# Quarter-wise loading and a shared k loop for the first two units of a hybrid decoder's input projection

## What is computed

```python
def rmsnorm(x, g):
    return x * lax.rsqrt(jnp.mean(x * x, axis=-1, keepdims=True) + EPS) * g

z = rmsnorm(x, norm_g) @ w_in               # (256 x 1024) @ (1024 x 3080)
q, k, v, o, gi, gf = jnp.split(z, [nq, 2 * nq, 2 * nq + nv, 2 * nq + 2 * nv,
                                   2 * nq + 2 * nv + A_HEADS], axis=-1)
li = softcap(gi + bf[:A_HEADS])                      # input gate, log
lf = jax.nn.log_sigmoid(softcap(gf + bf[A_HEADS:]))  # forget gate, log
# then, per head: cumulative sums of lf, running maxima, exp, and the chunked mixer
```

## Time and profile before

| | |
|---|---|
| median of 3 runs | 766.49 us (765.99 to 766.7) |
| the profiled execution's own time | 766.79 us |
| its span, first to last instruction | 765.1 us |
| PE busy | 752.0 us, 98% of the span |
| PE weight loads busy | 739.6 us, 97% |
| DVE, ACT, POOL busy | 537.5, 457.3, 228.7 us |
| mean granted TensorE clock | 0.994 |
| HBM traffic | 134.54 MB read, 177 GB/s over the span |

### The profile page before, as it was taken

How to read it: one execution, slowest core, us unless ns; L and a number is a source line. 1 busy time by engine, 2 the same in 40 slices (tenths; PEclk the granted TensorE clock), 3 DMA queues, 4 the chain that set the end, 5 groups by cost and what they waited for, 6 DMA issues and landing times.

```text
span 765.1 us, 16972 instructions
## 1 busy us (share of the span) xinstructions
PE 752.0 (98%) x6454; PEld 739.6 (97%) x6454; DVE 537.5 (70%) x993; ACT 457.3 (60%) x605; POOL 228.7 (30%) x186
## 2 busy tenths in 40 slices
PE   8999999999999999999999999999999999999995
PEld 7999999999999999999999999999999999999994
DVE  5784788888888546547746855766788888887452
ACT  6644557665666456448648637746867666665451
POOL 2350235432222522222322321320214222233321
PEclk9999999999999999999999999999999999999998
DMA  9754264756564565854584285384545656554731
GB/s 288 224 170 131 90 201 157 247 167 207 178 218 153 192 197 174 258 164 145 167 252 127 90 278 153 114 253 132 181 140 190 195 193 208 176 179 143 238 100 55
DMA packets 139805, 136.24 MB, mean 178 GB/s; under 512 B 3585, under 2 KB 139089, under 8 KB 139764
## 3 DMA queue, kind: packets, MB, share of 16 engines
q1 hardware_dynamic: 129016, 130.15, 52.7%
q10 hardware_dynamic: 10748, 5.53, 2.8%
HBM read 134.54 MB, written 1.13 MB: 177 GB/s over the span
## 4 chain that ended last, share of the span: by engine, by line
PE 92%; DVE 3%; issue 1%; ACT 1%; DMA 1%; ACTq 0%; POOL 0%; POOLq 0%; DVEq 0%
PE bank L1367 16%; PE bank L1369 15%; PE bank L1368 15%; PE banks L1368 9%; PE banks L1369 9%; PE banks L1367 9%; PE bank L1594 3%; PE bank L1596 3%; PE bank L1595 3%; PE banks L1628 2%; PE banks L1639 2%; PE bank L1399 1%; PE bank L1401 1%; PE bank L1400 1%; DVE wlo L875 1%
## 5 line engine op out<-in xcount | busy, mean ns | idle before, releaser
L472 POOL TENSOR_TENSOR wlo<-raw,whi 128x512 fp32r<-128x512 f32 (+1 forms) x165 | 218.5, 1357 | 501.7 <-ACT whi L515 501.7
L515 ACT ACTIVATE whi<-raw 128x2048 fp32r<-128x2048 f32 (+1 forms) x135 | 238.1, 1764 | 180.1 <-PE bank L1369 92.9
L875 DVE TENSOR_TENSOR wlo<-raw,whi 128x1024 fp32r<-128x1024 f32 x163 | 198.1, 1253 | 7.6 <-ACT whi L515 6.7
L1367 PE MATMUL bank<-xsA,whi 128*128 128x256 f32 x568 | 159.2, 280 | 0.0
L1368 PE MATMUL bank<-xsA,whi 128*128 128x256 f32 x568 | 157.7, 278 | 0.0
L1369 PE MATMUL bank<-xsA,wlo 128*128 128x256 f32 x568 | 157.6, 277 | 0.0
L1367 PE MATMUL bank<-xsB,whi 128*128 128x256 f32 x480 | 134.2, 280 | 0.3 <-DVE wlo L875 0.2
L1369 PE MATMUL bank<-xsB,wlo 128*128 128x256 f32 x480 | 132.6, 276 | 0.0
L1368 PE MATMUL bank<-xsB,whi 128*128 128x256 f32 x480 | 132.6, 276 | 0.0
L1367 PEld LDWEIGHTS bank<-xsA,whi 128*128 128x128 f32 x568 | 107.4, 189 | 1.4 <-DVE xsA L895 0.8
L1368 PEld LDWEIGHTS bank<-xsA,whi 128*128 128x128 f32 x568 | 107.5, 189 | 0.1
(11 more groups left out here) (202 smaller groups left out, 1521.8 us busy)
## 6 DMA issues: line engine op xcount, KB each, us to landing
raw<-in_f_w_up SPq DMA_DIRECT2D x44, 1024.0 KB, 5.1
raw<-in_w_kv SPq DMA_DIRECT2D x24, 1024.0 KB, 5.8
raw<-in_f_w_down SPq DMA_DIRECT2D x16, 1024.0 KB, 5.2
raw<-in_b_w_q SPq DMA_DIRECT2D x12, 1024.0 KB, 5.3
raw<-in_a_w_in SPq DMA_DIRECT2D x10, 1024.0 KB, 5.9
raw<-in_f_w_down SPq DMA_DIRECT2D x8, 768.0 KB, 4.8
Bi<-bias_by_distance ACTq DMA_DIRECT2D x16, 320.0 KB, 4.7
raw<-in_a_w_out SPq DMA_DIRECT2D x4, 1024.0 KB, 5.4
```

The source lines that it names most:

```text
L472: o = g.tensor_tensor(wlo[s][:, ka:kb, :], raw[s][:, ka * CW:kb * CW] .rearrange("p (k c) -> p k c", c=CW), whi[s][:, ka:kb, :].bitcast(F3 ...
L515: o = a.activation(whi[s][:, k0:k1, :], raw[s][:, k0 * CW:k1 * CW] .rearrange("p (k c) -> p k c", c=CW), ACT.Copy)
L875: v.tensor_tensor(wlo[s][:, ka:kb, :], raw[s][:, ka * CW:kb * CW].rearrange("p (k c) -> p k c", c=CW), whi[s][:, ka:kb, :].bitcast(F32), A ...
L1367: t_.matmul(ps, hi_w, hi_x, start=first, stop=False)
```

## The change

- X, unit 0 and unit 1 arrive in quarters of two blocks, in turn (12 loads of 256 KB). ACT and DVE split each quarter when it is there, of both units.
- PE does both units for each block k: 12 matmuls per k, tiles 0 to 3 in banks 0, 1, 2 and 5. Behind them come the sums, then the gate projection, then the bias table.
- The bias table is one matmul, its two left operands and its two right operands being stacked (`om`, `rg`). Their loads, that of `bif` and that of most of `vcols` go on SP behind unit 2's; ACT loads only the eight gain columns of layer 0.
- Unit 2 goes to banks 6 and 7. The first half of its wlo is made by DVE, the second by POOL; all of unit 1's is DVE's.
- WARM is 10. DVE's gate inputs go from unit 2 to unit 1, ahead of unit 3's wlo; the gate scans go ahead of the emptying of both of unit 3's tiles.

```diff
-WARM = 18
+WARM = 10
 PIECE = 2
-SHARE = 7
...
         def in_bank(t):
-            return 5 if t == 3 else t % 3
+            return {3: 5, 4: 6, 5: 7}.get(t, t % 3)
...
+            for j in range(4):
+                sp.dma_start(X[:, 2 * j:2 * j + 2, :], xT[:, 2 * j:2 * j + 2, :])\
+                    .then_inc(x_in[j], 16)
+                sp.dma_start(*cols_k(0, 2 * j, 2 * j + 2))\
+                    .then_inc(first_in[j] if j < 3 else raw_in[0], 16)
+                sp.dma_start(*cols_k(1, 2 * j, 2 * j + 2))\
+                    .then_inc(second_in[j] if j < 3 else raw_in[1], 16)
...
             for u in range(2, 12):
-                if u == 4:
+                if u == 5:
                     sp.wait_ge(share_lo, 1)
                 load(U_IN + u, 0, 0, cols(w_in, u * CW), KD)
+                if u == 2:
+                    sp.dma_start(om[0:BUCKETS, :], onehot).then_inc(c_in, 16)
...
+                    sp.dma_start(bif[:, :], b_if).then_inc(bif_in, 16)
+                    sp.dma_start(vcols[:, V_KV:], vectors[:, V_KV:]).then_inc(v_in, 16)
...
-            lo(1, k0=SHARE)
-            lo(2)
+            lo(2, k0=KD // 2)
...
+            act.wait_ge(va_in, 16)
+            for j in range(4):
+                act.wait_ge(x_in[j], 16)
+                for k in (2 * j, 2 * j + 1):
                     gained(k, ((xsA, V_A),))
+                if j < 3:
+                    first_part(0, j, first_in[j], first_hi)
+                    first_part(1, j, second_in[j], second_hi)
+                else:
+                    hi(0, k0=6)
+                    hi(1, k0=6)
+                if j == 1:
+                    square_in_turn(0)
+                    square_in_turn(1)
+            for k in range(2, KD):
+                square_in_turn(k)
...
+            dve.wait_ge(va_in, 16)
+            for j in range(4):
+                dve.wait_ge(x_in[j], 16)
+                for k in (2 * j, 2 * j + 1):
                     gained(k, k, ((xsA, V_A),))
...
+                first_part(0, j, first_hi, first_lo)
+                first_part(1, j, second_hi, second_lo)
+                if j == 2:
+                    added(0)
+                    added(1)
+            for k in range(2, KD):
                 added(k)
...
             for u in range(12):
-                if u == 2:
+                if u == 1:
                     gate_inputs()
...
-                    if (u, c) == (3, 1):
+                    if (u, c) == (3, 0):
                         gate_scans()
...
+            for k in range(KD):
+                pe.wait_ge(xlo_done, k + 1)
+                for n, lo_part in ((0, first_lo), (1, second_lo)):
+                    if k == 6:
+                        pe.wait_ge(lo_done[n], 2)
+                    elif k % 2 == 0:
+                        pe.wait_ge(lo_part, k // 2 + 1)
+                    for c in range(2):
+                        cs = slice(c * P, (c + 1) * P)
+                        mm = three(bank[in_bank(2 * n + c)][:, 0:S], whi[n][:, k, cs],
+                                   wlo[n][:, k, cs], xsA[:, k, 0, :], xsA[:, k, 1, :], k == 0,
+                                   k == KD - 1)
...
+            sums(0, 7, True)
...
-            for u in range(12):
+            for u in range(2, 12):
                 t = 2 * u
...
+                waits = {2: [(acc_done, 8), (root_done, 1)], 3: [(ev_done, 1), (ev_done, 2)]}\
+                    .get(u, [(ev_done, t + c - 2) for c in range(2)])
```

More of the change, by code:

```diff
@@ L586, in _, with first_part @@
[L586 to L596, removed]
+            def first_part(n, j, landed, done):
+                act.wait_ge(landed, 16)
+                a.activation(whi[n][:, 2 * j:2 * j + 2, :], raw[n][:, 2 * j * CW:(2 * j + 2) * CW]
+                             .rearrange("p (k c) -> p k c", c=CW), ACT.Copy).then_inc(done, 1)
@@ L1386, in unit @@
                 for k, c in order:
[L1387 removed]
+                    if not begun and k - k0 >= KD // 2:
                         pe.wait_ge(lo_done[s], 2 * rnd(n, i, step) + 2)
@@ L1446, in _ @@
+            sums(0, 7, True)
+            pe.wait_ge(wgl_done, 1)
+            for k in range(KD):
+                for part in range(2):
+                    mm = t_.matmul(bank[3][:, 0:S], wg4[:, k, :, :].rearrange("p j c -> p (j c)"),
+                                   xsA[:, k, part, :], start=k == part == 0,
+                                   stop=k == KD - 1 and part == 1)
+            mm.then_inc(gates_ps, 1)
             pe.wait_ge(c_in, 64)
-            t_.matmul(bank[4][0:NG * BH, 0:DIST], rb[:, :], oh[:, :], start=True, stop=False)
@@ L1448, in _ @@
-            t_.matmul(bank[4][0:NG * BH, 0:DIST], gs[:, :], mk[:, :], start=False, stop=True)\
+            t_.matmul(bank[4][0:NG * BH, 0:DIST], rg[:, :], om[:, :], start=True, stop=True)\
                 .then_inc(bt_done, 1)
-            for u in range(12):
+            for u in range(2, 12):
                 t = 2 * u
-                if u == 1:
-                    pe.wait_ge(share_lo, 1)
-                waits = [(ev_done, t + c - 2) for c in range(2)]
-                if u == 1:
-                    unit(U_IN + 1, xsA, [in_bank(2), in_bank(3)], part=(0, 2))
-                    pe.wait_ge(wgl_done, 1)
-                    for k in range(KD):
-                        for part in range(2):
-                            mm = t_.matmul(bank[3][:, 0:S],
-                                           wg4[:, k, :, :].rearrange("p j c -> p (j c)"),
-                                           xsA[:, k, part, :], start=k == part == 0,
-                                           stop=k == KD - 1 and part == 1)
-                    mm.then_inc(gates_ps, 1)
-                    sums(0, 7, True)
+                waits = {2: [(acc_done, 8), (root_done, 1)], 3: [(ev_done, 1), (ev_done, 2)]}\
+                    .get(u, [(ev_done, t + c - 2) for c in range(2)])
```

124 lines of the change are left out of this document (53 added, 71 removed).

## The result

The changed kernel takes **769.50 us** (median of 7 runs, 768.43 to 770.28), the kernel before 766.62 us beside it (7 runs, 765.99 to 767.20): a ratio of 1.0035, 95% interval [1.0026, 1.0044]. It is slower by 2.9 us, 0.5 us beyond the forecast's range. Its profiled execution took 768.52 us with a span of 766.8, against 766.79 and 765.1. So the two traces show 1.73 us of the difference. The executions of the changed kernel lie in two groups, 768.4 to 768.8 (three, the profiled one among them) and 769.5 to 770.3 (four). Executions in the chip's slow state, which are over 1.5% above the fastest of their kernel (such as 833.8 and 1079 us), are left aside throughout.

What follows compares the result with a forecast made beforehand. PE, on 92% of the chain, bounds the kernel. Of 4.5 us won by unit 2, PE's 3.6 us wait leaves 0.9; a clock fall costs 1.6: 766.79 + 0.7 = 767.5, less 0.3 to the median, 767.2; range 763.3 to 769.0.

Steps and rivals of the forecast that it cites:

- The opening: Start to unit 2: data in quarters lets PE start at about 6.9 instead of 10.95; unit 2 begins 4.5 us earlier.
- T2: Moment at which PE begins unit 2: 26.43 us before the change, forecast 21.9 after it.
- the clock in the opening hardly matters: Opening: PE's matmuls end at 17.8, or 19.4 with a clock fall; sums wait for DVE's queue until 18.3.
- the later stages shift as they are: Behind the gate transposes: everything moves with them, with no gain or loss of its own.
- chance for "slower": Chance of a measured time above 768.0 us, given as 0.22.
- (c): Rival, 15%: clock low in the opening as well, PE's 96 matmuls end at 19.4, scans at 39.8; +2.1 us, 768.6.
- the forecast's 45%: Chance of the main case: PE's wait with a clock fall behind it, 767.2 us.
- The move of the scans: DVE's gate scans, from 31.6 to 39.0, precede emptying unit 3's first tile, so PE waits about 3.6 us.
- The wait: PE stands about 3.6 us before unit 4's second half, until bank 0 is emptied; resumes at 39.25.
- The clock behind the wait: After PE's 3.6 us wait before unit 4's second half the clock falls, costing 1.6 to 1.7 us.
- -0.9 + 1.6 = +0.7: Whole forecast: 0.9 us still won at unit 4's second half, 1.6 lost to a clock fall behind PE's wait.
- POOL's encounter with the scans: POOL's unit 5, from 31.7, meets DVE's gate scans as before; they take 7.4 us rather than 3.7.

Runs made afterwards that it cites:

- the filler: Changed kernel with 12 matmuls on ones, into bank 6, in front of PE's wait for bank 0: 768.59 us, ratio 1.0022.

## Why the prediction was wrong, point by point

**The opening: right in kind, 2.1 us short.** T2 was forecast at 21.9 and came at 24.03. PE's first real matmul was forecast at 6.9 and came at 7.57: the gain columns still landed only by 4.68, where ACT's first row waited 1.90 us for them, and the first quarter of the weights was not there when X was scaled (0.48 us).

```profile
4.68 0.91 ACT L532 ACTIVATE xsA<-X,vcols 128x256 fp32r<-128x256 f32 x2 [1.90 <-DMA vcols<-in_vectors]
6.07 1.36 ACT L579 ACTIVATE whi<-raw 128x512 fp32r<-128x512 f32 x2 [0.48 <-DMA raw<-in_a_w_in]
```

Of the 2.1 us, 0.9 remains without a clock fall: in the three kernels with WARM 18 the bias product starts at 21.71 to 21.86 and unit 2 at 22.70 to 22.84. There the sums start at 18.7 to 19.0 instead of 18.3, and sums, gates and bias product take 3.9 instead of 3.64; the late first matmul is no term of its own beside that. The other 1.2 is the opening's clock fall.

**The steps that failed.** The first is the sentence that the clock in the opening hardly matters. The forecast had PE's end at 19.4 with a fall against DVE's 18.3, so by its own numbers it did matter, by 1.1. DVE's chain was nearly right (its last addition ended at 18.6, or 18.85 in the kernel with the scans back); PE was the later one. With the fall the sums started at 20.16 and the reciprocal at 21.64; without it, in four kernels, they started at 18.7 to 19.0 and at 20.4 to 20.55 (forecast 20.15). DVE's queue from there on was as forecast, so the scans began at 33.03 instead of 31.6 and PE went on at 40.87 instead of 39.25. This step alone does not explain the time: with WARM 18 it is repaired, and the time is 769.07. The second is the sentence that the later stages shift as they are, a term of nothing that measured 0.85 us; more on it below.

**The readings and sums.** The forecast says that the granted clock is 1.00 at first. The column says so, but the warm-up's own records run at half pace until about 4.7 us, and how long they do differs by execution, which the forecast for WARM 10 left out. Its chance for "slower", the 15% of (c) and a tenth of the forecast's 45%, adds up to 0.20, not 0.22.

**The order of rivals.** Rival (c), the fall in the opening, had 15%, on an idle time of 1.6 us from 5.3 to 6.9. It was 2.14, and the place in the kernel before with 2.0 us idle and a fall behind it was the nearest one. (c) should have stood level with the forecast. That the longer idle time decided the branch is not shown: the warm-up's pace doubles at different moments too.

**The move of the scans: right.** From the reciprocal to the scans it took 11.4 us (21.64 to 33.03), forecast 11.5. They lasted 7.3, forecast 7.4; POOL began 0.3 us ahead of them, forecast 0.1 behind. The wait stands where it was said, released by the row it was said of: 2.80 us, forecast 3.6, less because PE itself got there 2.3 later (37.9 against 35.6) and went on only 1.6 later (40.87 against 39.25). The kernel with WARM 18 is the clean check of this part: 3.31 us of wait, a fall behind it, the transposes 1.65 us later than before, forecast 0.7. The difference is DVE's, not that of T2, which only shortens the wait:

```profile
31.85 0.67 DVE L1046 TENSOR_TENSOR_SCAN gn<-gones,gl 4x256 f32<-4x256 f32 x1
39.67 0.76 DVE L1123 TENSOR_TENSOR kT<-bank,rstd 128x256 f32<-128x256 f32 x2
```

The scans began 0.25 us late, took 7.8 us instead of 7.4, and PE went on 0.5 behind their end, where 0.25 was reckoned: 40.14 instead of 39.25.

**The clock behind the wait: right in some executions.** In the profiled one no fall followed 2.80 us of idle time, in two others (after 3.31 and 3.1) one did. That -0.9 + 1.6 = +0.7 for the early part is near the measured +0.85 is luck: the first term was 1.75 off, the second was absent. Where both stand, in the kernel with WARM 18, the time is 769.07.

**What no term held.** 0.43 us of PE's time behind 48 us (0.15 to 0.53 in the nine other kernels with the new opening, but 0.2 also in two edits of the kernel before) and 0.4 in the tail. The forecast took the later stages to shift as they are, and its upper bound, 769.0, held only the early part's unknowns; these 0.85 us are more than the 0.5 by which the median is outside. Of the median's 2.88 us, 1.73 are found in the two traces. Of the other 1.15, 0.17 is the profiled execution of before standing above its median, and 0.98 that of the changed kernel standing below its own. That this last part is clock falls behind the wait, in executions without a trace, is not shown, and the mean granted clock does not speak for it: it is 0.993 in all seven executions, where one more stretch of 3.4 us at half speed would take off an estimated 0.002 (1.7 of 767), unless the low stretch at the end of the program were shorter by as much.

**By the Trainium skill.** The Trainium skill's GPSIMD Engine Reference, Specifications, names contention between GpSimd and VectorE instructions with two SBUF inputs. The forecast took it as scans of 7.4 us instead of 3.7, and the trace agrees: 7.3, against 3.7 in the kernel with POOL held back. SBUF — State Buffer, Who interferes with whom, in the Trainium skill goes further: it calls the shared port pair an exclusive lock, and says of DVE's 2-port modes that whoever issues first has the pair for the whole instruction. The rows agree with a lock as far as DVE goes: in the changed kernel each of the four that met a POOL piece was 0.8 to 1.0 us longer. A smaller share is seen only where the first scan began late in POOL's first piece, 1.04 us with the filler and 0.83 with the scans back and the old banks, in place of 0.67.

## What to carry to other kernels

When a change brings an engine's start forward, look for what the same change puts in front of a buffer's release: here the eight small scans before one emptying cost more than the whole opening gave, and the same scans one tile later cost 0.3 us. A delay that is free in one place, as POOL's encounter with the scans was, has to be priced again wherever the operations move. And fewer warm-up matmuls are no saving when they only lengthen the time that PE stands idle: eighteen in place of ten narrowed the spread from 2.2 to 0.5 us and gave the lowest time.

## What the runs showed of the hardware

- **Where tiles stand in SBUF.** 64 bytes of shift of X's parts, `wlo` and all tiles behind them against `whi` and `raw` slowed the matmuls from 0.113 to 0.118 us, 18.8 us in all, with no wait and the clock at 1.00. An edit that adds a small tile in the middle of an arena can do this, as here.
- **One DVE operation per POOL piece.** A scan, a two-input operation or a cast on 4 partitions takes 0.27 to 0.68 us alone and 1.24 to 1.81 when it meets a piece of POOL's subtraction, four times in each of nine traces, whichever of the eight were hit. In two more traces three were hit in full and the first scan in part.
- **The idle time and the clock.** In the opening a fall followed in all six traces with 2.00 to 2.32 us of idle PE, and none followed in five with 0.50 to 1.67; in the one with 1.90 the pace was low from the start. At the bank waits none followed 2.80, 1.97 or 1.04, and one followed 3.1 and 3.31. The work ahead of the two places differs, and so does, by execution, the moment between 4 and 7 us at which the warm-up's pace doubles. Idle time alone does not say whether the clock falls.
- **The clock column before its first change** can read 1.00 while PE does six matmuls a microsecond. Count the records.
